# Two transformer blocks in float32: the PE taps of a depthwise convolution in groups of four on shifted copies of 32 channels, and the first expert's transposes moved ahead of the second gather

## The reference

```python
h = rmsnorm(x, norm_mix_g) * (1 + sc1) + sh1          # sc1, sh1 from c @ ada_w
u = h @ w_in + b_in
a, gt = jnp.split(u, 2, axis=-1)
u = a * jax.nn.sigmoid(gt)
y = lax.conv_general_dilated(u, w_dw[:, None, :], window_strides=(1,),
    padding=[(CONV_WIDTH - 1, 0)], dimension_numbers=('NWC', 'WIO', 'NWC'),
    feature_group_count=D_MODEL) + b_dw                # each channel with its own 31 weights
y = jax.nn.silu(layernorm(y, ln_g, ln_b))
x = x + g1 * (y @ w_out)
h = rmsnorm(x, norm_ffn_g) * (1 + sc2) + sh2
x = x + g2 * hier_moe(h, ...)    # per expert: (silu(xb @ w_gate[e]) * (xb @ w_up[e])) @ w_down[e]
```

## Time and profile before

| | |
|---|---|
| median of 3 runs | 952.25 us (952.18 to 952.89) |
| the profiled execution | 952.4 us, its span 950.4 us |
| TensorE busy | 910.1 us, 96% of the span |
| VectorE, ScalarE, GpSimd busy | 278.7, 208.1, 197.2 us |
| gated product and convolution | about 41 to 106 us of the span |
| experts | about 165 to 619 us |

### The profile page before, as it was taken

The page is one execution under the profiler, slowest core; times in us unless marked ns, Lnnn a source line. Parts: engine busy times, 40 slices in busy tenths (PEclk is TensorE's granted clock), DMA queues, the critical chain, the costliest instruction groups (busy, mean ns, idle before and its releaser), DMA issues.

```text
span 950.4 us, 13285 instructions
## 1 busy us (share of the span) xinstructions
PE 910.1 (96%) x5200; PEld 538.9 (57%) x5200; DVE 278.7 (29%) x734; ACT 208.1 (22%) x497; POOL 197.2 (21%) x327
## 2 busy tenths in 40 slices
PE   7999999999999999989889899999999999999996
PEld 5788686544443444434334344388766658688544
DVE  3399724311101110010010101144035446260334
ACT  3355524211110111001010011032215501011640
POOL 0287300121111111111111110032003302023221
PEclk9999999999999999999999999999999999999999
DMA  9997975879999999999999999992400943402001
GB/s 363 425 424 323 382 288 209 339 321 418 428 428 429 426 427 428 427 428 428 428 427 428 427 425 422 428 419 83 177 2 1 398 174 148 177 1 90 1 1 44
DMA packets 23962, 286.12 MB, mean 301 GB/s; under 512 B 2658, under 2 KB 3426, under 8 KB 5090
## 3 DMA queue, kind: packets, MB, share of 16 engines
q1 hardware_dynamic: 23184, 283.99, 72.0%
q10 hardware_dynamic: 722, 1.33, 0.4%
HBM read 284.26 MB, written 1.05 MB: 300 GB/s over the span
## 4 chain that ended last, share of the span: by engine, by line
PE 73%; DMA 18%; DVE 6%; issue 1%; ACT 1%; SPq 1%; POOL 0%; POOLq 0%; DVEq 0%
PE bank L989 18%; PE bank L1233 18%; DMA arena<-in_w_expert_up 15%; PE bank L1250 8%; PE bank L1454 5%; DVE bank L1706 5%; PE bank L1260 4%; PE bank L1401 3%; DMA arena<-in_w_ada 2%; PE bank L1433 2%; PE bank L1221 1%; PE bank L1467 1%; PE bank L1592 1%; PE bank L1418 1%; PE bank L1479 1%
## 5 line engine op out<-in xcount | busy, mean ns | idle before, releaser
L1233 PE MATMUL bank<-arena 128*64 128x512 f32 x1024 | 226.4, 593 | 19.4 <-DMA arena<-in_w_expert_up 19.2
L989 PE MATMUL bank<-arena 128*128 128x256 f32 (+1 forms) x992 | 211.1, 373 | 0.6 <-ACT arena L840 0.4
L989 PEld LDWEIGHTS bank<-arena 128*128 128x128 f32 x992 | 183.2, 190 | 27.1 <-issue 3.4
L1233 PEld LDWEIGHTS bank<-arena 128*64 128x64 f32 x1024 | 78.5, 137 | 162.8 <-issue 162.6
L1250 PE MATMUL bank<-arena 128*64 128x512 f32 x512 | 116.9, 598 | 0.8 <-ACT arena L810 0.8
L1903 DVE TENSOR_TENSOR arena<-bank,arena 64x512 f32<-64x512 f32 x32 | 21.8, 683 | 273.1 <-ACT arena L806 273.0
L810 ACT ACTIVATE arena<-bank 128x512 f32<-128x512 f32 x32 | 19.1, 598 | 376.9 <-PE bank L1242 376.9
L1250 PEld LDWEIGHTS bank<-arena 128*64 128x64 f32 x512 | 34.1, 136 | 66.3 <-issue 65.5
L567 POOL COPY der<-arena 128x4 f32 (+1 forms) x30 | 5.6, 188 | 314.5 <-PE bank L1242 295.9
L1260 PE MATMUL bank<-arena 64*128 64x256 f32 x512 | 65.8, 386 | 0.6 <-DVE arena L1921 0.5
L1706 DVE SCALAR_TENSOR_TENSOR bank<-arena,par,bank 128x256 f32<-128x256 f32 x143 | 58.3, 482 | 0.6
(11 more groups left out here) (255 smaller groups left out, 843.1 us busy)
## 6 DMA issues: line engine op xcount, KB each, us to landing
arena<-in_w_expert_down SPq DMA_DIRECT2D x32, 2048.0 KB, 29.8
arena<-in_w_expert_gate SPq DMA_DIRECT2D x26, 2048.0 KB, 26.1
arena<-in_w_expert_up SPq DMA_DIRECT2D x26, 2048.0 KB, 30.6
arena<-in_w_ada SPq DMA_DIRECT2D x12, 2048.0 KB, 32.3
arena<-in_w_expert_gate SPq DMA_DIRECT2D x12, 1024.0 KB, 19.8
arena<-in_w_expert_up SPq DMA_DIRECT2D x12, 1024.0 KB, 21.4
arena<-in_w_kv SPq DMA_DIRECT2D x4, 2048.0 KB, 14.9
arena<-in_w_in_b SPq DMA_DIRECT2D x4, 2048.0 KB, 8.0
```

Source lines behind the costliest of these rows:

```text
L989: mm = pe.matmul(bank[part:part + m, at:at + n], w[:, k, lo:lo + m], rhs[:, k0 + k, :], start=(i == 0), stop=(i == tiles - 1))
L1233: mm = pe.matmul(GU_BANK[half * WIN:(half + 1) * WIN, :], xw[b][:, k, :], w[:, k, :], start=(k == 0), stop=(k == KD - 1), skip_group_check ...
```

## The change

Four taps become one group of products. For tile j and each block g of 32 channels, four transfers copy the block's rows of `u`, shifted by 0, 1, 2 and 3 tokens, to the four 32-partition blocks of an area, 16 transfers of 32 rows for a tile. One product of 128 rows by 32 columns then adds four taps of 32 channels; four of them, one for each g, write the four quarters of the tile. `PE_SLOTS` gives the number of such groups: one for tiles 0 to 4, two for tiles 5 to 7 (the second reads the same area 4 tokens further). The taps on VectorE follow from it. The areas `a`, `b`, `c`, `h` are used again by later tiles. The copies are issued by SyncE between its loads. GpSimd makes the diagonals from a folded identity, one 128x128 product for each group. The last tile's turn on TensorE moves behind tile 5, `ada(6, 2)` ahead of tile 5. In the experts, `turn(0)` moves ahead of the second gather, its bank is 3 in place of 2, and the banks of the second gather are dealt so that bank 3 is free.

```diff
-PE_TAPS = (3, 3, 3, 3, 3, 3, 3, 5)
+FOLD = 4
+FOLDED = P // FOLD
+PE_SLOTS = (1, 1, 1, 1, 1, 2, 2, 2)
+PE_TAPS = tuple(FOLD * n for n in PE_SLOTS)
+SECOND = PE_SLOTS.index(2)
...
-PE_ORDER = (0, 1, 2, 3, 4, LAST, 5, 6)
+PE_ORDER = (0, 1, 2, 3, 4, 5, LAST, 6)
...
-        diag = area(R, DIAGS, P)
+        diag = arena[:, R:R + DIAGS * P].rearrange("p (d g n) -> p d g n", d=DIAGS, g=FOLD)
+        fold_ident = arena[:, R + 1856:R + 1856 + FOLDED]
+        FOLD_AT = (("a", R + 2032), ("b", R + 3072), ("c", R + 9456), ("a", R + 2032), ("b", R + 3072), ("a", R + 2032),
+                   ("h", R + 4112), ("b", R + 3072))
...
+        def folded(j):
+            return area(FOLD_AT[j][1], FOLD, fold_columns(j))
+
+        def fold_landed(j):
+            name = FOLD_AT[j][0]
+            return sem(f"fold_{name}"), 16 * FOLD * FOLD * sum(FOLD_AT[i][0] == name for i in range(j + 1))
...
-                plan(("gather", half, j), 1 + (KD * half + j + 5) % 7)
+                plan(("gather", half, j), (7, 1, 2, 4, 5, 6, 7, 1)[j] if half else 1 + (j + 5) % 7)
...
-        GU_BANK, Y_BANK, T_BANK = ps[0], ps[1], ps[2]
+        GU_BANK, Y_BANK, T_BANK = ps[0], ps[1], ps[3]
...
+            def fold(j):
+                lo, n = FOLD_AT[j][1], fold_columns(j)
+                moved(sp, ("glu_a", j))
+                earlier = [i for i in range(j) if FOLD_AT[i][0] == FOLD_AT[j][0]]
+                if earlier:
+                    sp.wait_ge(sem("diag_used"), sum(PE_SLOTS[i] for i in PE_ORDER[0:PE_ORDER.index(earlier[-1]) + 1]))
+                if j > SECOND:
+                    filled(sp, ("glu_g", KD - 1))
+                for g in range(FOLD):
+                    for i in range(FOLD):
+                        sp.dma_start(arena[FOLDED * i:FOLDED * (i + 1), lo + g * n:lo + (g + 1) * n],
+                                     u[FOLDED * g:FOLDED * (g + 1), j, i:i + n]).then_inc(fold_landed(j)[0], 16)
+
+            folds = {13: (0, 1), 14: (2, 3, 4), 15: (5,), 16: (6,), 17: (7,)}
             for i in range(5, CHUNKS_A):
                 if i >= RING:
                     filled(sp, chunks[i - RING][3])
                 load(i)
+                if i == 13:
+                    sp.wait_ge(sem("u_edge"), 1)
+                for j in folds.get(i, ()):
+                    fold(j)
...
-                for w in range(PE_TAPS[j]):
+                for q in range(PE_SLOTS[j]):
                     if made >= DIAGS:
                         pool.wait_ge(sem("diag_used"), made - DIAGS + 1)
-                    pool.tensor_scalar(diag[:, made % DIAGS, :], ident, col("conv_w_dw", w * KD + j), 0.0,
-                                       ALU.mult, ALU.add).then_inc(sem("diag_ready"), 1)
+                    pool.tensor_tensor(diag[:, made % DIAGS, :, :], fold_ident.unsqueeze(1).broadcast_to((P, FOLD, FOLDED)),
+                                       fold_weights(j, q).unsqueeze(2).broadcast_to((P, FOLD, FOLDED)),
+                                       ALU.mult).then_inc(sem("diag_ready"), 1)
                     made += 1
...
+            move_turned(t_full, C_T + 1, 0, t_moved)
             for j in range(0, KD, 2):
                 gathered(1, j)
-            move_turned(t_full, C_T + 1, 0, t_moved)
...
+                pe.wait_ge(*fold_landed(j))
+                for q in range(PE_SLOTS[j]):
                     pe.wait_ge(sem("diag_ready"), made[0] + 1)
-                    mm = pe.matmul(to, diag[:, made[0] % DIAGS, :], u[:, j, w:w + T],
-                                   start=(j == LAST and w == 0), stop=False, skip_group_check=True)
+                    for g in range(FOLD):
+                        mm = pe.matmul(to[FOLDED * g:FOLDED * (g + 1), :], diag[:, made[0] % DIAGS, g, :],
+                                       folded(j)[:, g, FOLD * q:FOLD * q + T], start=(j == LAST and q == 0), stop=False,
+                                       skip_group_check=True)
                     mm.then_inc(sem("diag_used"), 1)
                     made[0] += 1
...
             convolve(4)
             ada(4, 2)
+            ada(6, 2)
+            convolve(5)
             convolve(LAST)
-            convolve(5)
             ada_columns(4, 0, 2, 2 * P)
-            ada(6, 2)
             convolve(6)
...
             for e in range(BODY):
                 begin(e, e, lambda s, back: EXPERT_BASE[s] + 16, first=e == 0)
+                if e == 1:
+                    pe.wait_ge(sem("bank3_read"), BEFORE_EXPERTS[3])
+                    turn(0).then_inc(t_full, 1)
                 if e < 2:
                     gather(e)
```

More of the change, by code:

```diff
@@ L79 @@
            ("conv_b_dw", 8), ("conv_ln_g", 8), ("conv_ln_b", 8), ("c", 8), ("mla_q_norm_2", 6),
-           ("mla_kv_norm_2", 2), ("ln_g_2", 16), ("ln_b_2", 16), ("conv_w_dw", TAPS * KD)]
+           ("mla_kv_norm_2", 2), ("ln_g_2", 16), ("ln_b_2", 16), ("conv_w_dw", TAPS * KD),
+           ("conv_w_fold", FOLD * sum(PE_SLOTS))]
 COL = {}
@@ L133, in two_blocks, with fold_columns, fold_weights @@
         sg = area(R + 10480, 4, T)
-        diag = area(R, DIAGS, P)
+        diag = arena[:, R:R + DIAGS * P].rearrange("p (d g n) -> p d g n", d=DIAGS, g=FOLD)
+        fold_ident = arena[:, R + 1856:R + 1856 + FOLDED]
+        FOLD_AT = (("a", R + 2032), ("b", R + 3072), ("c", R + 9456), ("a", R + 2032), ("b", R + 3072), ("a", R + 2032),
+                   ("h", R + 4112), ("b", R + 3072))
+        def fold_columns(j):
+            return T + FOLD * (PE_SLOTS[j] - 1)
+        def fold_weights(j, q):
+            at = COL["conv_w_fold"] + FOLD * (j if q == 0 else KD + j - SECOND)
+            return par[:, at:at + FOLD]
+        def folded(j):
[3 more added lines that the diff above has]
+            return sem(f"fold_{name}"), 16 * FOLD * FOLD * sum(FOLD_AT[i][0] == name for i in range(j + 1))
         cact = area(R + 12288, KD, 32)
@@ L160, in two_blocks @@
         hid = arena[0:WIN, R + 6144:R + 6144 + HIDDEN]
-        turned_e = [arena[:, R + 10240 + b * 512:R + 10752 + b * 512] for b in range(BODY)]
+        turned_e = [arena[:, R + 10240 + b * 512:R + 10752 + b * 512] for b in (2, 0, 1)]
         hid_t = [a[:, 0:KF * WIN].rearrange("p (f n) -> p f n", f=KF) for a in turned_e]
@@ L531, in _ @@
             made, added = 0, 0
+            for g in range(1, FOLD):
+                left = ident[:, 0:FOLDED] if g == 1 else fold_ident
+                if g > 1:
+                    pool.wait_ge(sem("fold_ident"), g - 1)
+                pool.tensor_tensor(fold_ident, left, ident[:, g * FOLDED:(g + 1) * FOLDED], ALU.add) \
+                    .then_inc(sem("fold_ident"), 1)
+            pool.wait_ge(sem("fold_ident"), FOLD - 1)
             for c in range(KD):
                 j = PE_ORDER[c]
-                for w in range(PE_TAPS[j]):
+                for q in range(PE_SLOTS[j]):
                     if made >= DIAGS:
                         pool.wait_ge(sem("diag_used"), made - DIAGS + 1)
-                    pool.tensor_scalar(diag[:, made % DIAGS, :], ident, col("conv_w_dw", w * KD + j), 0.0,
-                                       ALU.mult, ALU.add).then_inc(sem("diag_ready"), 1)
+                    pool.tensor_tensor(diag[:, made % DIAGS, :, :], fold_ident.unsqueeze(1).broadcast_to((P, FOLD, FOLDED)),
+                                       fold_weights(j, q).unsqueeze(2).broadcast_to((P, FOLD, FOLDED)),
+                                       ALU.mult).then_inc(sem("diag_ready"), 1)
                     made += 1
@@ L1075, in convolve @@
             def convolve(j):
-                n = PE_TAPS[j]
                 if j == LAST:
@@ L1084, in convolve @@
                 moved(pe, ("glu_a", j))
-                for w in range(n):
+                pe.wait_ge(*fold_landed(j))
+                for q in range(PE_SLOTS[j]):
                     pe.wait_ge(sem("diag_ready"), made[0] + 1)
-                    mm = pe.matmul(to, diag[:, made[0] % DIAGS, :], u[:, j, w:w + T],
-                                   start=(j == LAST and w == 0), stop=False, skip_group_check=True)
+                    for g in range(FOLD):
+                        mm = pe.matmul(to[FOLDED * g:FOLDED * (g + 1), :], diag[:, made[0] % DIAGS, g, :],
+                                       folded(j)[:, g, FOLD * q:FOLD * q + T], start=(j == LAST and q == 0), stop=False,
+                                       skip_group_check=True)
                     mm.then_inc(sem("diag_used"), 1)
@@ L1299, in finish @@
                 if e != EXPERTS - 1:
-                    pe.wait_ge(hid_ready, e)
-                    turn(b1).then_inc(t_full, 1)
                     if not second:
+                        pe.wait_ge(hid_ready, e)
+                        turn(b1).then_inc(t_full, 1)
                         pe.wait_ge(y_moved, e - 1)
@@ L2180, in laid_out @@
 def laid_out(a):
+    taps = np.concatenate([a["conv_w_dw"][0][0:FOLD].reshape(FOLD, KD, FOLD, FOLDED),
```

(2 more changed lines are left out.)

## The result

The changed kernel takes 1002.3 us (median of 6 runs; the kernel before 952.85 beside it), a ratio of 1.051 [1.050, 1.053]: 5% slower. One run of the six took 3299.7 us and is left out of the comparison; no trace of it was kept, and its cause is open. The profiled execution took 1000.75 us with a span of 998.7. The direction was forecast, the size was not: 980, with a range to 992.

The account below looks back on a forecast made before the run. TensorE and what it waits for bound the kernel, with the transfers' queue deciding. 952.4 us plus 27.8 for the later mean plus 0 for the transposes gave 980.2, say 980; bounds 973 to 985.5, range 970 to 992.

Parts of the forecast that it names:

- a shift of the mean: Mean over the channels, at 106.22 us before the experts: any delay there delays the end equally; forecast 27.8 us later.
- Tile 0's copies: Convolution's start: copies queue behind a load issued at 40.9 us, land at 80.0, needed at 55.37; TensorE stalls 24.6 us.
- The clock: TensorE's granted clock falls during each of two idle times, before tile 0 and near the last tile; 2.0 us lost each.
- The groups, columns and sums: TensorE's work after the last copy lands: 3.0 us of products plus 2.0 of clock loss before the mean.
- The transposes: First expert, moved ahead of the second gather: one wait replaces another at the first down product; 0, bounds -0.8 and +0.3 us.
- Rival A: Transfers' queue: copies pass the loads, landing 2 us after issue, no stall before the tail; 951.4 us, chance 0.15.
- rival B: Copies cost more each, in issue or landing: 988 us at 0.65, 999 at about 1, 1031 at 2; chance 0.13.
- Issue: successive issues stand 0.37 us apart: SyncE's queue: issuing each small copy takes 0.40 us, 6.4 us a tile; bounds 0.33 and 0.50.
- Copies of tiles 2 to 5 are in time by the same rates: Middle of the convolution: these copies land before TensorE needs them, tile 5's issued by 113 us and needed at 121.
- the tail: Last two tiles: SyncE issues their copies after glu(7), the last lands at 129.0 us; TensorE waits 6.4 us.
- Moving ... I take 1.9: Transfers' queue: moving one tile's 512 small packets takes 1.9 us, between 1.2 by bytes and 2.3 at most.
- the pace: TensorE on tiles 0 to 4 after the stall: 7.79 us a tile, 0.84 less than 8.63, against VectorE's 7.6.

## Why the prediction was right or wrong

**Right.** The kernel is bounded by TensorE and what it waits for, and a shift of the mean is a shift of the end: 48.4 and 48.3 us. Tile 0's copies stood behind load 13: the stall ran to 84.2 where 80.0 was forecast, and the two runs that changed place and number apart (2.70 us with other places, 27.33 with half the number) show place as its cause. The clock fell in both stalls. The groups, columns and sums between the last landing and the mean took 5.2 us (149.44 to 154.65) where 5.0 was said. The transposes were worth nothing, with VectorE's read as the new wait: 0.64 us in the trace, and 1.000 in the run of that part alone. Rival A, copies that pass the loads, fell by its own test: none landed before 76.8 us. The first ones did come 3.8 us ahead of the load before them, which was no part of the forecast. Nor was the landing time of a small transfer paid in turn, rival B at its extreme: a copy landed 1.8 to 1.9 us after its issue, and the next was issued 0.63 us behind it.

**Wrong: the issue.** The step that failed is "Issue: successive issues stand 0.37 us apart ... I take 0.40: 6.4 us a tile; bounds 0.33 (an issue alone) and 0.50". It measured 0.63 with an empty queue; in the kernel 0.65 to 0.70 from 81.85 us on and 1.23 for the first 32 copies, behind the loads: 102.9 us for all 128, 0.80 each, outside both bounds. The rows it rested on the earlier trace rows are all loads from memory, and the run of transfers alone shows that this matters: 0.46 with one end in memory, 0.63 with both ends in the chip. What the kernel took beyond 0.63 it took mostly for the first 32 copies, with the queue full.

**And what followed from it:** "Copies of tiles 2 to 5 are in time by the same rates". At 0.40 a copy, 96 copies behind 81.85 us are 38 us and SyncE waits for glu(7) at 113.2, as I said. At 0.66 they are 63 us, SyncE never waits for glu(7), and SyncE itself is the chain from 41.9 to 147.7. I followed the tiles through the queue at 0.40 only, and let a dearer issue, in the bounds as in rival B, lengthen just the two tiles of the tail. The whole queue against the stage would have shown it: 128 x 0.63 is 81 us of issue, and from the last modulation load to the mean there were 65 (40.9 to 106.2). Rival B had the right price for 96 of the copies, 0.65, and a time of 988 that is 14 us below the median measured for the same reason: it charged 32 copies. (Rival A's 954.4 for 0.50 an issue should be 954.6 by its own terms, which changes nothing.)

The 20.6 us between the mean forecast, 134.0, and the mean measured, 154.65, divide so on TensorE's timeline:

| term | forecast | measured | adds |
|---|---|---|---|
| tile 0's products begin | 80.0 | 84.2 | 4.2 |
| from there to glu(7) done | 33.2 | 34.55 | 1.35 |
| from glu(7) to the last tile's products | 15.8 (landing) | 30.7 | 14.9 |
| from there to the mean | 5.0 | 5.2 | 0.2 |

The first term is a size: the mechanism held. Of its 4.2 us, 0.6 is a later start of this execution (load 13 issued at 41.48, not 40.9), and the rest the term "Moving ... I take 1.9": from the first copy's landing, 76.8, to the sixteenth's, 84.0, a tile's copies took 7.2 us beside the end of load 13, where they were to follow it within 2. The second is the pace, 8.1 us and not 7.79, and the clock: the first `glu` after the stall took 8.28 us against 7.07 later. The third is the failed step. It alone decided: the chain runs over SyncE's issue and not over tile 0's stall, so with the first two terms as forecast and the issue as it was, the last copy would have landed no earlier. The forecast put the whole 24.6 us of stall on the way to the mean; the stall came, but the issue beside it took longer.

**Where the gain went.** TensorE took 0.5 us a tile less (8.63 to 8.1), not the 0.84 forecast: the group took 0.57 and not 0.45, the sum 0.53 and not 0.43, the `glu` products 7.00 and not 6.91. It was never visible in the time, since the issue of the copies set the mean.

## What to carry to other kernels

Price a transfer by its issue as well as its bytes, with rows of the same two ends: sixteen small copies inside the chip cost the engine that issues them 10 us, and more while its queue is full. Before moving work from an engine to a queue, add up every issue of the stage against the length of the stage, not only those at its end. A small transfer behind a single large load waits for the load (2.4 us became 7.6), so dealing loads evenly between small urgent transfers puts a load ahead of each; the small ones belong ahead of the loads, or where the queue has run empty.

## What the runs showed of the hardware

The issue of a transfer with both ends in the chip takes 0.63 us on SyncE and on ScalarE, at 32 or 128 rows, at 1 KB or 128 bytes a row; with one end in memory 0.45 to 0.46 where the queue was empty. With the queue full, single issues of copies took up to 3.0 us; tile 0's and tile 1's 32 took 39.3 us to issue, against 21.3 with five loads fewer ahead of them and 20.2 at the empty queue's rate. A small copy can land shortly before the load issued ahead of it in the same queue (76.8 against 80.6 us in the change, 27.2 against 27.9 in the transfers alone), and in no run earlier than that. A tile of copies needed 19.8 to 19.9 us beside 6 MB of loads whether it stood behind them in the same queue or in another, though the first copy came at 16.4 us in the one and at 6.5 in the other.
